# Starting a projection while its input arrives, and reordering the sample stage of a decoder-trunk kernel

## The reference

```
u = rmsnorm(x, g_pre) @ w_in           # w_in 1024 x 4384, split into
                                       # q_m k_m v_m o_m z_m (512 each), i_m f_m (4 each), q_n (512),
                                       # kv_cmp kv_sel kv_win (256 each), g_n (24), z_n (512)
h_m = mlstm(silu(conv(q_m, k_m)), v_m, i_m + b_i, log_sigmoid(f_m + b_f)) * sigmoid(o_m)
o_n = g0 * attend(q, compressed kv) + g1 * attend(q, 16 selected blocks of 64) + g2 * attend(q, window of 512)
y = x + rmsnorm(concat(h_m * silu(z_m), o_n * silu(z_n)) @ w_out, g_post)
```

## Time and profile before

| | us |
|---|---|
| median of 3 runs | 1059.21 (1059.05, 1059.21, 3899.0) |
| the profiled execution's own time | 1056.59 |
| its span, first to last instruction | 1054.8 |
| mean granted TensorE clock in it | 0.993 of full |
| busy: PE, PEld, DVE, ACT, POOL | 1020.5, 613.9, 473.7, 338.0, 70.1 |

### The profile page before, as it was taken

One profiled execution on the slowest core, in us unless ns is written; L12 is line 12 of the kernel. 1 busy time (PEld: TensorE's weight loads), 2 busy tenths in 40 slices (PEclk: granted clock), 3 DMA queues, 4 the chain that ended last, 5 costly groups with the idle time before them and its releaser, 6 DMA issues.

```text
span 1054.8 us, 14571 instructions
## 1 busy us (share of the span) xinstructions
PE 1020.5 (97%) x5289; PEld 613.9 (58%) x5289; DVE 473.7 (45%) x1170; ACT 338.0 (32%) x816; POOL 70.1 (7%) x178
## 2 busy tenths in 40 slices
PE   7999999999999999999999899999999899899997
PEld 6766654444445555578676455665655778345443
DVE  5644441100122222223244888787885565353542
ACT  6321120000001111111113777777776632122220
POOL 1000000000000001111102110100200520000000
PEclk9999999999999999999999899999999999999999
DMA  9402020030403114143101300000020768433412
GB/s 314 198 2 80 0 80 0 7 97 0 83 1 97 25 36 104 35 125 64 61 1 29 107 26 1 1 2 1 9 74 2 183 174 255 141 120 123 157 43 83
DMA packets 83165, 77.49 MB, mean 73 GB/s; under 512 B 28354, under 2 KB 67566, under 8 KB 83030
## 3 DMA queue, kind: packets, MB, share of 16 engines
q1 hardware_dynamic: 71478, 61.82, 19.8%
q10 hardware_dynamic: 11616, 14.74, 5.3%
HBM read 66.59 MB, written 14.10 MB: 77 GB/s over the span
## 4 chain that ended last, share of the span: by engine, by line
PE 87%; SPq 5%; DMA 2%; DVE 2%; issue 2%; ACT 1%; DVEq 0%; ACTq 0%
PE PS L2197 29%; PE PS L2190 16%; PE PS L2435 9%; PE PS L2267 7%; PE PS L2280 6%; PE PS L2252 6%; PE PS L1997 1%; SPq L723 1%; SPq L739 1%; SPq L732 1%; DMA WR<-in_w_out 1%; PE PS L2009 1%; PE PS L2464 1%; PE PS L2154 1%; DMA out_s_C<-GM 1%
## 5 line engine op out<-in xcount | busy, mean ns | idle before, releaser
L2197 PE MATMUL PS<-WR,XT 128*128 128x512 f32 (+1 forms) x768 | 306.9, 557 | 0.0
L2197 PEld LDWEIGHTS PS<-WR,XT 128*128 128x128 f32 x768 | 144.0, 190 | 147.7 <-issue 144.6
L2190 PE MATMUL PS<-XT,WR 128*128 128x352 f32 x576 | 172.7, 460 | 0.0
L2190 PEld LDWEIGHTS PS<-XT,WR 128*128 128x128 f32 x576 | 108.5, 190 | 58.9 <-issue 0.4
L2252 PE MATMUL PS<-KTR,XT 64*128 64x512 f32 (+3 forms) x352 | 71.1, 509 | 0.0
L1211 ACT ACTIVATE XT<-XT 128x640 f32<-128x640 f32 (+7 forms) x96 | 69.8, 730 | 2.8 <-DVE XT L1666 2.7
L2267 PE MATMUL PS<-cst,XT 128*128 128x128 f32 x396 | 64.7, 287 | 5.2 <-DVE XT L1677 3.9
L1666 DVE CUSTOM_DVE_ANT_1 XT<-PS,KVN 128x640 f32<-128x640 f32 (+6 forms) x84 | 62.1, 764 | 16.7 <-PE PS L2252 16.6
L2267 PEld LDWEIGHTS PS<-cst,XT 128*128 128x128 f32 x396 | 42.3, 141 | 41.8 <-issue 18.5
L2435 PE MATMUL PS<-WR,KT 128*128 128x512 f32 x128 | 61.7, 604 | 2.5 <-DMA WR<-in_w_out 2.5
L2435 PE MATMUL PS<-WR,QT 128*128 128x512 f32 x128 | 61.2, 599 | 0.0
(11 more groups left out here) (472 smaller groups left out, 1221.4 us busy)
## 6 DMA issues: line engine op xcount, KB each, us to landing
WR<-in_w_in SPq DMA_DIRECT2D x24, 512.0 KB, 8.2
WR<-in_cache_kv_cmp SPq DMA_DIRECT2D x56, 128.0 KB, 2.5
MT<-row_factors ACTq DMA_DIRECT2D x16, 256.0 KB, 7.6
WR<-in_w_in SPq DMA_DIRECT2D x32, 128.0 KB, 3.3
QN<-in_cache_kv_win SPq DMA_DIRECT2D x8, 512.0 KB, 6.0
out_s_kv_win<-in_cache_kv_win SPq DMA_DIRECT2D x1, 4064.0 KB
out_y_prompt<-MT ACTq DMA_DIRECT2D x7, 512.0 KB, 2.9
XT<-in_x_prompt ACTq DMA_DIRECT2D x6, 512.0 KB, 4.2
```

The source lines that it names most:

```text
L2190: ins = mm(b[:, 0:THIRD], w[:, k, r // 3 * P:(r // 3 + 1) * P], xt[:, k, r % 3 * THIRD:(r % 3 + 1) * THIRD], **f)
L2197: ins = mm(b[:, 0:width], xt[:, k, r * P:(r + 1) * P], w[:, k, :], **f)
```

## The change

1. *Head.* x is turned in halves of 64 rows: sixteen 64 x 128 transposes for a tile, each into 64 columns. Tile 0 to 2 are turned first, tiles 3 to 8 in the middle of the first three products of q_m, after the fourth and the eighth slice. DVE scales tiles 1 and 2 after it has copied tile 0. The first feature tile of w_in (`w_first`) is loaded after x tile 2, the other three after all of x. q_m's first six tiles run over two feature tiles alternately (`column_tile`), so that each third of the tokens is used twice. PE is given 29 products of a zero tile (`warm`) around the first transposes. The gate columns are packed into 32 and multiplied once, ahead of q_m's fifth tile, by column tiles (`gate_products`). Their forget rows reach their place by a DMA that SP issues after ACT has copied the gates out.
2. *Numerators.* The eight products of 4 columns become eight by column tiles of 32 with 128 columns (`qblk`, a block diagonal of q that DVE fills for each head). ACT copies the sum out, and one more product with a constant matrix gathers the four partial rows (`numerators`).
3. *Order of the sample part.* POOL sorts sequence 3 ahead of the rotations. DVE does `sum_sample(2)` and the second half of `sum_sample(4)` earlier. PE turns one pair of sequence tiles ahead of each head. The products of the ninth set have banks 3 and 6 and are split around `turn_values(7)`.
4. *SP.* The page numbers of sequences 0 to 3, 6 and 7 are held from before the sample part. The two rereads there fall away (those of the four sequences of the second pass stay). `load_wo(6)` and `load_wo(7)` go ahead of the loads of x for the residual.

```diff
 def weights_in(g):
-    return 16 * sum(2 * KC if GROUPS[m][0] in ("q_n", "z_n") else 4 for m in range(g % 2, g + 1, 2))
+    return 16 * sum(2 * KC if GROUPS[m][0] in ("q_n", "z_n") else 4 if m else 3 for m in range(g % 2, g + 1, 2))
+def column_tile(u, third):
+    return 2 * third + u if u < 2 else 3 * u + third
...
 # SP
-            sp.wait_ge(zeros_ready, 3)
-            for row, c0, width in ((MROW_I, C_I, 2 * MH), (MROW_G, C_G, 3 * NH)):
-                sp.dma_start(wmisc[:, :, row:row + width], w[:, :, c0:c0 + width]).then_inc(wmisc_in, 16)
+            sp.dma_start(w0[:, :, 0:P], w[:, :, 0:P]).then_inc(w_first, 16)
             for i in range(3, NT + 1):
                 load_x(i)
+            for u in range(1, 4):
+                sp.dma_start(w0[:, :, u * P:(u + 1) * P], w[:, :, u * P:(u + 1) * P]).then_inc(w_in_s[0], 16)
+            for row, c0, width in ((0, C_I, 2 * MH), (2 * MH, C_G, 3 * NH)):
+                sp.dma_start(wmisc[:, :, row:row + width], w[:, :, c0:c0 + width]).then_inc(wmisc_in, 16)
...
-            load_w(0)
             load_w(1)
+            sp.wait_ge(gate_rows, 1)
+            sp.dma_start(fp, raw_rows[MH:2 * MH, :]).then_inc(wmisc_in, 16)
...
-            held = [[page(4 + j, n) for n in range(NPG)] for j in range(4)]
+            held = {b: [page(b, n) for n in range(NPG)] for b in (0, 1, 2, 3, 6, 7)}
...
-                        src = I["cache_kv_sel"][0, bass.ds(held[j // 2][n] if j % 2 == 0 else page(j, n), 1), :, :, :, :]
+                        src = I["cache_kv_sel"][0, bass.ds(held[j][n], 1), :, :, :, :]
...
             load_cmp(7)
-            held = [[page(j, n) for n in range(NPG)] for j in (0, 2)]
...
             load_windows(0, (2, 3))
+            sp.wait_ge(cmp_done, 2 * SB + 1)
+            load_wo(6)
+            sp.wait_ge(cmp_done, 2 * (SB + 1))
+            load_wo(7)
             sp.wait_ge(num_done, MH)
             for i in range(2):
                 sp.dma_start(xr[:, i, :], xf[i * P:(i + 1) * P, :]).then_inc(xr_in[i], 16)
-            sp.wait_ge(cmp_done, 2 * (SB + 1))
-            load_wo(6)
-            load_wo(7)
...
 # ACT, head
+            for third in range(2):
+                for u in range(2 - third):
+                    take_third(u, third)
+            act.wait_ge(gate_done, 1)
+            for j in range(4):
+                nc.scalar.activation(by_tile(raw_rows, j), by_bank(bank(0, 2)[32 * j:32 * j + 2 * MH, :]), ACT.Copy)
+            for j in range(4):
+                ins = nc.scalar.activation(by_tile(gt_rows, j), by_bank(bank(0, 2)[32 * j:32 * j + 32, :]), ACT.Tanh, scale=0.5)
+            ins.then_inc(gate_rows, 1)
...
+            take_third(1, 1)
             act.wait_ge(gates_in, 1)
...
             act.wait_ge(gates_in, 4)
...
-            take_third(0, 2)
+            take_third(1, 2)
...
 # DVE, sample part
+            sum_sample(2, (0,))
             dve.wait_ge(f_act, 2)
...
+            sum_sample(2, (1,))
...
             link(tt(wts[0:NS, :], bank(7)[0:NS, 192:192 + P], ds_[0:NS, :], ALU.mult))
+            sum_sample(4, (1,))
             dve.wait_ge(f_pe, 4)
             tt(n_new[0:SB, :], n_new[0:SB, :], bank(3)[0:SB, :], ALU.add).then_inc(f_dve, 1)
-            sum_sample(4, (1,))
...
 # PE, head
+            pe.wait_ge(zeros_ready, 2)
+            warm(8)
+            pe.wait_ge(x_in[0], 2 * 16)
+            pe.wait_ge(params_in, 5 * 16)
+            nc.tensor.transpose(bank(4)[:, 0:48], par_rows[0:48, :], ident[0:48, 0:48]).then_inc(x_turned, 1)
+            warm(6)
+            turn_x(0)
+            warm(10)
+            turn_x(1)
+            turn_x(2)
+            warm(5)
...
+            def gate_products():
+                pe.wait_ge(xt_ready, NT + 1)
+                pe.wait_ge(wmisc_in, 2 * 16)
+                for i0 in range(0, NT, 4):
+                    for k in range(KC):
+                        for j in range(4):
+                            t = (i0 + j) * P
+                            ins = mm(bank(i0 // 4)[32 * j:32 * j + 32, 0:P], wmisc[:, k, :], xt[:, k, t:t + P], start=k == 0, stop=k == KC - 1)
+                ins.then_inc(gate_done, 1)
...
+                    if g == 0 and r == 0:
+                        pe.wait_ge(xt_ready, 3)
+                        pe.wait_ge(w_first, 16)
+                    if g == 0 and r == 1:
+                        pe.wait_ge(w_in_s[0], weights_in(0))
+                    if g == 0 and r == 2:
+                        pe.wait_ge(xt_ready, 6)
+                    if g == 0 and r == 4:
+                        gate_products()
...
+                            if g == 0 and r < 3 and k % 4 == 3:
+                                turn_x(3 + 2 * r + k // 4)
...
 # PE, heads of the sample group
+            def numerators(h):
+                pe.wait_ge(f_act, 6 + h)
+                x = bank(6)[:, h * NS:(h + 1) * NS]
+                mm(x, us_all[0:NS, 3, h * P:(h + 1) * P], wts[0:NS, h * NS:(h + 1) * NS], start=True, stop=False)
+                mm(x, num_s, s_col(S_SAME, NS), start=False, stop=True)
...
-                mm(x[:, 0:NS], v[0:NS, :], wts[0:NS, h * NS:(h + 1) * NS], start=True, stop=True)
+                if h:
+                    numerators(h - 1)
                 for b in range(SB):
-                    ins = mm(x[:, P + b * ST:P + (b + 1) * ST], cts[h % 2][:, b, :],
-                             qis[:, h * NS + b * ST:h * NS + (b + 1) * ST], start=True, stop=True)
+                    ins = mm(bank(7)[b % 4 * NS:(b % 4 + 1) * NS, 0:P], qblk[:, b * NS:(b + 1) * NS], cts[h % 2][:, b, :],
+                             start=b < 4, stop=b >= 4)
```

More of the change, by code:

```diff
@@ L137, in first_tile @@
 def first_tile(g):
-    return MISC + sum(TILES[:g])
+    return sum(TILES[:g])
 def tile_of(n):
@@ L834, in _ @@
                 sp.dma_start(xr_s[r, :], xs[:, c]).then_inc(gp_in, 16)
-            held = [[page(4 + j, n) for n in range(NPG)] for j in range(4)]
+            held = {b: [page(b, n) for n in range(NPG)] for b in range(4, SB)}
             sp.wait_ge(kb_turned, 8)
@@ L980, in _ @@
             pool.wait_ge(s_rot, 3)
-            for b in range(3, SB):
+            for b in range(4, SB):
                 sort_sample(b)
@@ L1026, in _ @@
             act.wait_ge(zeros_ready, ZEROS)
[L1027 to L1035 removed]
             def take_third(u, third):
[L1039 to L1041 removed]
+                n = column_tile(u, third)
+                act.wait_ge(proj_done, n + 1)
+                b, t = bank(4 + n % 4), third * THIRD
                 w = min(THIRD, T - t)
@@ L1292, in _ @@
             take_sample(5, (2, 3))
+            take_sample(6, (0, 1))
             def load_wo(c):
@@ L1404, in _ @@
                                         op0=ALU.mult).then_inc(x_scaled, 1)
-                if i == 1:
-                    take_parameters()
-                if i:
+            take_parameters()
+            scale_in(0)
+            turn_in(0)
+            scale_in(1)
+            scale_in(2)
+            turn_in(1)
+            turn_in(2)
+            for i in range(3, NT + 1):
+                scale_in(i)
+                if i > 3:
                     turn_in(i - 1)
@@ L1988, in _, with turn_x @@
             mm = nc.tensor.matmul
-            pe.wait_ge(consts_in, 16)
-            def gate_rows(i):
-                pe.wait_ge(xt_ready, i + 1)
-                if i == 0:
-                    pe.wait_ge(zeros_ready, ZEROS)
-                for k in range(KC):
-                    ins = mm(bank(4 + i // 4)[:, i % 4 * P:(i % 4 + 1) * P], wmisc[:, k, :], xt[:, k, i * P:(i + 1) * P],
-                             start=k == 0, stop=k == KC - 1)
-                if i % 4 == 3:
-                    ins.then_inc(proj_done, 1)
-            for i in range(NT + 1):
-                rows = P if i < NT else NS
+            def turn_x(i):
+                rows = 64 if i < NT else NS
                 pe.wait_ge(x_scaled, i + 1)
@@ L2008, in _, with warm @@
                 for k in range(KC):
-                    ins = nc.tensor.transpose(bank(i % 2 * 2 + k // 4)[:, k % 4 * rows:(k % 4 + 1) * rows],
-                                              xa[i][0:rows, k * P:(k + 1) * P], ident[0:rows, 0:rows])
+                    for half in range(2 if i < NT else 1):
+                        r = slice(64 * half, 64 * half + rows)
+                        ins = nc.tensor.transpose(bank(i % 2 * 2 + half)[:, k * rows:(k + 1) * rows],
+                                                  xa[i][r, k * P:(k + 1) * P], ident[r, r])
                 ins.then_inc(x_turned, 1)
-                if i == 0:
-                    pe.wait_ge(params_in, 5 * 16)
-                    nc.tensor.transpose(bank(4)[:, 0:48], par_rows[0:48, :], ident[0:48, 0:48]).then_inc(par_turned, 1)
-                else:
-                    gate_rows(i - 1)
-            pe.wait_ge(xt_ready, NT + 1)
+            def warm(n):
+                for _ in range(n):
+                    mm(bank(7)[:, 0:P], g4[:, 0:P], g4[:, 0:P], start=True, stop=True)
```

(11 more changed lines are left out.)

155 lines of the change are left out of this document (83 added, 72 removed).

## The result

| | before | after |
|---|---|---|
| median of the runs | 1059.13 us | 1043.55 us (1041.75 to 1045.97) |
| ratio | | 0.9876, 95% interval 0.985 to 0.9901 |
| profiled execution, own time | 1056.59 us | 1042.63 us |
| its span | 1054.8 us | 1040.8 us |

The four runs before are 1058.67, 1059.05, 1059.21 and the far-off 3899.0 us. The ratio is not the quotient of the two medians, which is 0.9853 (a gain of 15.6 us). By the ratio the gain is 13.1 us (10.5 to 15.8), from a base of 1056.7; not all runs behind that base are listed here. The 42 runs of the kernel before that were timed with the experiments, on three chips, have a median of 1055.39 us (1051.62 to 1062.79).

A forecast was written before the change was run, and what follows sets the result against it. PE, busy nearly the whole span, was taken as the bound. Head 6.3 us plus sample part 11.2 us gave 17.5 us off 1059.21, so 1041.7, stated as 1041.5 us, range 1033 to 1051.

The forecast's parts named there:

- Sort and sum_sample(2): Sample part: PE's 2.19 us idle before L2112 goes, but it then meets a wait on DVE; about 0.9 us gained.
- sum_sample(4): Sample part: 1.98 us of PE idling goes by DVE summing earlier and a moved pair of transposes; 2.0 us gained.
- Numerators: Sample heads: column-tile products save 0.9 us for each of four heads, less 0.6 at the third; 3.0 us gained.
- Ninth set: Sample part: the ninth set's products fill 1.27 us of PE idling; 1.3 us gained.
- w_out and its clock: End of sample part: earlier SP removes PE's wait on w_out's last rows, 2.53 us, and the half clock, 1.5 us.
- start of q_m: Head: q_m's first product begins at 15 us instead of 34.83, or at 16 if zero products don't raise the clock.
- later than 18 us: Sign for the head: the prediction is wrong if L2190's first row, q_m's start, comes after 18 us.
- the weights' wait: Head, q_m's second tile: PE idles 1.5 us for w_in's first 512 columns, landing at 23 us; possibly 3 more.
- Turned tiles: Head, inside q_m: turning x tiles 3 to 8 costs 0.9 us each, 5.1 us in all (bounds 3.5 and 10).
- The wait at the tenth tile: Head, q_m: PE idles 1.8 us for a bank until ACT copies tile 5 out after the last gate exponential.
- The clock behind that wait: Head: 0.5 us taken off the gain for the chance that the clock falls in one of two waits.
- rule on tiling modes: Head and numerators: each mode change drains TensorE, some 0.2 us a block, 2.4 us over twelve, already contained in the terms.

The follow-up runs named there:

- sample undone: Changed kernel with SP's two edits, PE's numerators and the POOL and DVE orders put back; head, moved transposes and ninth set kept: 1055.12 us, ratio 0.9989.
- second tile's weights: On top of gates early: weights of q_m's second 128 columns before x tiles 5 to 8, tile 0 before the parameters, fewer zero products: 1034.62 us, 0.9813.
- the second run, copy early: Changed kernel with only ACT's copy of tile 6 moved ahead of the last three steps of gate exponentials: 1042.26 us (one run).
- gates early: Changed kernel with the gate products in front of q_m's fourth tile instead of the fifth: 1038.55 us, ratio 0.982.
- no zero products: Changed kernel with the four calls of `warm` taken out: 1043.11 us, ratio 0.9884.
- old numbers: Changed kernel with SP reading page numbers as the kernel before did, instead of holding them in registers: 1050.25 us, ratio 0.9953.
- old numerators: Changed kernel with only PE's numerators back to sixteen instructions per head, the state as stationary operand: 1047.82 us, ratio 0.9935.
- SP as before: Changed kernel with SP's page-number reads and the place of w_out's last rows both as in the kernel before: 1052.64 us, ratio 0.9976.

## Why the prediction was right, and where it was off

I said 1041.5 us, range 1033 to 1051, and 17.5 us of gain; the median is 1043.55. The gain is smaller than the 2 us between these two times suggest: the marks give 15.3 for head and sample part, the ratio 13.1 in all, three quarters of the forecast. The time came out near because the 17.5 were taken from 1059.21, a base 2.6 us above that of the ratio. That part is luck.

*The sample part, 11.2 us forecast, 11.04 measured.* It is the part where every term had a row. Sort and sum_sample(2): 0.9 forecast; from L2353 to L2424, 3.81 us earlier against 2.92 at the start of the part, so 0.89. sum_sample(4): 2.0; the first head comes 4.81 us earlier with a pair of transposes (0.9) more ahead of it, so 1.9, of which the order of the sums is 0.96 by its own run. Numerators: 3.0; the loop is 2.6 shorter (L2489, 7.41 earlier, less the 4.81), and PE's old form put back costs 3.2. The new form (0.64 us for 16 instructions) is the 0.65 that I took. Ninth set: 1.3; between the loop's end and L2557 another 2.15 us are gained, of which 0.9 is the pair of transposes, so 1.2. w_out and its clock: 2.53 + 1.5; the rest, 13.96 − 9.56 = 4.4. The reason given for the last one needs a correction. I had the registers free w_out. The runs show that they free the last page first (4.79 us when undone) and w_out second. Without the registers the whole sample part gains 3.35 us (98.24 for 101.59), so it is not a term by itself: undone with the heads fast it costs 7.7 us, with slow heads (sample undone) no page is late and the wait is 2.39 us on w_out, as the 2.53 in the kernel before.

*The head, 6.3 us forecast, 4.24 measured*, by its own terms. The step that was off is the start of q_m, forecast at 15 us and 2.05 late. It had two errors. I took tile 0 as scaled by 7.1 us, from rows of the kernel before; in the changed kernel DVE's list has the parameters ahead of it. They are the last of five small DMAs and reach PE at 7.47 us, so tile 0 is scaled at 9.22. And I wrote "the zero products end before the transposes need PE, and cost nothing there". Six of them at half pace (2.93 us) follow the parameters, and tile 0 is turned at 10.56, 1.3 us after it could have been. Without them q_m began at 15.82, 1.2 us earlier, of which 0.5 is an earlier landing of the parameters (at PE 6.95): so about 0.7 of the 2.05 us is the zero products', and the rest stands with the parameters and DVE's order behind them. With both changed, tile 0 was turned at 7.29 and q_m began at 15.12 (second tile's weights). My sign of being wrong, "later than 18 us", was met in three other profiles of the same head order (18.05, 18.66 and 19.05 us; the range of all is 16.49 to 19.05). There k_m began at 89.0 to 90.0, inside the spread of the others, so the sign said little about the gain. The error was hidden, since the weights' wait, 1.5 in the forecast, shrank to 0.15: they landed at 23.57, as worked out (23). Turned tiles cost 0.83 each where I took 0.9, with the short one 5.0 for 5.1. Gates 4.12 for 4.6. The wait at the tenth tile 2.03 for 1.8, with the reason as given; tile 11 had no slack, as the second run showed. The clock behind that wait cost 1.7 in this profile where I took 0.5. But it is not a fixed price: ten runs have this idle time, 2.02 to 2.04 us each; in three of them the three tiles behind it take 16.16 us, in seven 14.47. The mean is 0.5.

*Of the rule on tiling modes* the runs show both sides. The Trainium skill (TensorEngine Tiling, Key Properties) has it that a change of mode drains TensorE, and the trace agrees: a half tile takes 2.56 us between turned tiles where 2.375 is usual, so the two edges of a turned tile cost 0.19 us together, as worked out. In whole transposes the half tile is at 2.37, and the gain of the shorter 64-row form (0.64 for 0.87 us) is nearly eaten by the edges: 3.21 against 3.24 us.

*What stays open: the middle.* On PE it is the same code in all runs, and it took 722.64 to 729.31 us. (The changed kernel's additional reads of page numbers on SP stand behind 600 us.) The difference is half clock between 565 and 600 us. Windows there (granted clock is the third number from the end) of the second tile's weights, then of the kernel before, then of the sample undone:

```profile
580.00:590.00 10.00, 9.71 (x66) 5.55 (x64) 9.24 (x36) 7.80 (x30) 1.70 (x4) 1.00 0.39 108
```

```profile
580.00:590.00 10.00, 8.38 (x42) 4.66 (x40) 7.17 (x39) 6.51 (x27) 1.04 (x1) 0.68 0.34 103
```

```profile
580.00:590.00 10.00, 8.39 (x32) 4.12 (x32) 6.22 (x35) 5.80 (x24) 1.04 (x1) 0.59 0.37 105
590.00:600.00 10.00, 10.00 (x51) 5.51 (x50) 7.46 (x31) 6.07 (x22) 1.55 (x4) 0.73 0.37 107
```

Against the run that stayed at full clock, the kernel before lost 2.5 us here and eleven of the other twelve more than that, up to 6.7. If this were chance alone, medians of four to nineteen runs would average it out. They don't quite: marks and timed ratios agree with the gates early (18.5 by head and sample part, 19.0 timed) and nearly with the second tile's weights (21.0 and 19.7), but the timed gain is 2 to 4.5 us less than head and sample part give in the changed kernel (15.3 and 13.1), no zero products, old numbers, old numerators, SP as before and sample undone (5.7 and 1.2). For the changed kernel and no zero products the marks still lie just inside the ratio's interval, for the other four outside it (with SP as before only just). The mean granted clock, which is on record for every timed run, points the same way. It is 0.994 over the 42 runs of the kernel before (the fastest, 1051.62 us, at 0.998, the slowest, 1062.79, at 0.988), 0.996 with the gates early and 0.994 with the second tile's weights, but 0.991 in the changed kernel, 0.993 without zero products, 0.990 with the old numerators, 0.988 with the old numbers and with SP as before, and 0.986 with the sample undone. A hundredth of the clock over the whole time is some 10 us (an estimate: 0.01 x 1050). So the kernels with the gates where the change put them lost more clock on average than the kernel before, and the two with the gates earlier didn't. Part of that is the half clock that their profiles show behind q_m's tenth tile and in the sample part. For the rest the profiles point to the start of attention, but a timed run doesn't say where it lost its clock, there is one profile of the kernel before, and no run varied that stretch; why it is lost there stays open.

## What to carry to other kernels

When a chain runs over several engines (gates here, from PE over ACT and DVE back to PE's banks), moving one engine's step within it shifts the wait to the next tile; moving the chain's start by one tile removed it for 0.5 us. A freed queue is worth what its next late transfer allows, so cost it together with the edits that make its consumer faster, not alone. For a change of one per cent, compare marks in the trace that bound identical code: here the clock of an untouched stretch moved the total by up to 6.7 us.

## What the runs showed that I had not expected

- Half clock (1.2 of 2.4 GHz) doesn't follow an idle time of PE surely: behind the same 2.03 us it came in three of ten runs. Behind the 1.72 us ahead of the sample part's second step it came in four of the eleven runs that have that wait, and with the old numerators it came at 856 us, where PE had not idled since 846.
- The granted-clock column can miss it. With the copy early the window from 8 to 14 us shows 1.00, though twelve instructions of zero products take 2.93 us there and ten take 1.38 at 16.51 us. Durations of equal instructions decide.
- Weights in pieces of 512 bytes moved at 293 GB/s from 17 to 20 us, with the queues busy at a share of 1.22, where x moved at 410 from 12 to 14. Issuing them held SP: one issue took 5.44 us. The gate columns behind them, in pieces of 32 and 96 bytes, moved at 83 GB/s from 22 to 23 us. Placing one piece of the weights before the last x tiles left PE without a wait at its second tile (21.53).
- SP's reads of page numbers cost about 0.5 us a page when they stand at the DMA (8.45 us for eight pages, against 4.79 with held numbers for the same eight).
